# Regrouping the token-major mixer projections of a two-layer encoder kernel into pieces of 512, 512, 512 and 192 columns, with two more matrix-product buffers moved and a few orders changed

## The chip, the cores and the metric

The kernel runs on one core of a Trainium2 chip. The metric is the device time of one execution in microseconds (us), smaller is better. All times below are device times or times from one profiled execution.

## The reference

The input is 256 tokens of 1024 features in float32, with 256 memory tokens. Two layers follow one another; each is a token mixer, a cross-attention into the memory tokens and a gated feed-forward block. Cut to what matters here, the mixer is:

```python
proj = h @ w_in                       # 256 x 1024 times 1024 x 3800-odd
(ml_q, ml_k, ml_v, ml_o, ml_g, na_q, na_k, na_v,
 g_q, g_k, g_v, g_g, g_a) = jnp.split(proj, pts, axis=-1)
# six mLSTM heads of 64: ml_h from ml_q, ml_k, ml_v and the gates ml_g
ml_out = head_rms_norm(ml_h, ml_norm_g, 6) * sigmoid(ml_o)
# five neighbourhood-attention heads from na_q, na_k, na_v
# five gated-linear-attention heads from g_q, g_k, g_v, g_a
gla_out = head_rms_norm(gla_h, gla_norm_g, 5) * silu(g_g)
mixed = concat([ml_out, na_out, gla_out]) @ w_out
```

Five of the thirteen parts of `proj` are wanted with tokens on the partitions ("token-major"): `ml_v` and `ml_o` (384 columns each), `na_v`, `g_v` and `g_g` (320 each), 1728 columns in all.

## The kernel before

**Split products.** Every weight and every activation of a large product is held as a high part and a low part, and a product is three TensorE matmuls (high by high, high by low, low by high). A weight *unit* is up to 2048 values per partition. The DMA queue of SyncE (SP) brings it into one of three slots `raw`; ScalarE (ACT, line 1250) rounds it to `whi`; VectorE (DVE, line 1640) subtracts to get `wlo`; TensorE (PE, lines 755 to 757) uses both. SP may load unit u only when the low half of unit u-3 is done (`load`, line 603 is its DMA); ACT may write `whi` of unit u only when TensorE has used unit u-3. The order of units is the list that `layer_units` writes, and SP, ACT, DVE and TensorE all go through it in that order, each at places of its own program written out by hand (`ahead` on ACT and on DVE, `between` on DVE, `ML_FILL` and `NA_FILL` on TensorE).

**Token-major products.** `tm_half` multiplies half of the 1024 input features (unit `a` or `b`, four blocks of 128) for both groups of 128 tokens: 24 matmuls with the activations stationary and n columns moving. `tm_unit` does both halves, 48 matmuls. The pieces are v 384, nv 320, gv 320, o 384 and gg 320 columns.

**The mLSTM heads.** TensorE makes v, then loops `hh` over the six heads. In step hh it does head hh-1's output (`ml_output`, line 963, which waits until DVE has drained `mls{hh-1}`), in even steps the scores of two heads (line 976), and then a *fill*: nq, nk, gk, nv, gv, o. For each head DVE adds decay rows (lines 1798 to 1801, "decay steps" below), ACT takes the exponential (line 1395), DVE multiplies the scores by it (lines 1814 to 1817, "multiply steps") and TensorE can make the output. The decay rows of head 0 come from a TensorE bank; those of heads 1 to 5 make a round trip through memory: SP waits for the scan (`scan_ready`), writes `gA` out (line 636), waits for `rows_out`, and reads a broadcast row back for each head (line 640). This block stands in SP's loop ahead of the load of unit `nva`:

```python
if name == "nva":
    sp.wait_ge(scan_ready, l + 1)
    sp.dma_start(a["rows"][l], gA[:, :]).then_inc(rows_out, 16)
    sp.wait_ge(rows_out, 16 * (l + 1))
    for hh in range(1, MLH):
        ...
        sp.dma_start(decay_row(hh), ...).then_inc(rows_in[hh], 16)
```

DVE's step for head hh from 1 on begins with `dve.wait_ge(rows_in[hh], ...)`.

**After the heads.** DVE sums the mLSTM heads (`heads_sum`, lines 1777 to 1782), multiplies the decays (`decayed`, lines 1761 and 1762), and then serves the neighbourhood heads: maxima of `nas` (line 1879), shares (`shares_of`, lines 1861 and 1863), then the split of the first memory-key unit (`xk0` in layer 0, `xk2` in layer 1) and the low halves of the memory tokens (`memory_lo`, line 1676). TensorE makes nas, gg, the transposes `nat0` (line 1002, waits for `shares_of(0)`), and then the key unit, whose first blocks wait for the low half of the weights, for each `memory_lo` and for its bank. The bank is 7, and gg's first tokens (`gg0`) were in it, so it waits for ACT to have drained them. SP issues 16 small copies of `nav` (line 633) ahead of the load of that key unit.

**Further on.** `ga` and `kv` products, then xv0 (memory values) into banks 0 and 1, of which bank 0 held `ga0`, drained by DVE at line 1918. In the cross-attention TensorE does transposes `xt3` (line 1150) between the outputs `xo_1` and `xo_2` (line 1161).

Of the kernel before, what the change touches and what calls it, by code (L numbers as in the profile page):

```python
# [21 lines left out]
P = 128  # L22
# [30 lines left out]
def layer_units(l):  # L53
# [16 lines left out]
    tm("v", "w_in", C_V, ML)  # L70
# [42 lines left out]
ML_FILL = (("nq",), ("nk",), ("gk",), ("nv0", "nv1"), ("gv0", "gv1"), ("o0", "o1"))  # L113
WIDTH = {"v": ML, "nv": NA, "gv": GV, "o": ML, "gg": GV}


def layer_events(l):
# [29 lines left out]
    for h in range(MLH + 1):  # L147
        if h:
            job(f"mlo{h - 1}", 4 + (h - 1) % 2)
        else:  # L150
            job("mlb0", 2)
        if h < MLH and h % 2 == 0:
            job(f"mls{h}", 0)
            job(f"mls{h + 1}", 1)
        if h < MLH and len(ML_FILL[h]) == 1:
            job(ML_FILL[h][0], (7, 6)[h % 2], ML_FILL[h][0])
        elif h < MLH:
            tm(ML_FILL[h][0][:-1], (7, 6))
    for h in range(NAH + 2):
# [8 lines left out]
        if h == 0:  # L168
            tm("gg", (7, 6))
# [10 lines left out]
    job("xv0_0", 0)  # L180
    for i in range(4):
        job(f"go{i}", 2 + i)
    job("xv0_1", 1, "xv0b")
# [9 lines left out]
    for kind, i in XATTN:  # L193
        if kind == "xq":
            job(f"xq{i}", (0, 1, 6, 7)[i], f"xq{i}")
        elif kind != "xq_begun":
# [20 lines left out]
for _l in range(1, DEPTH):  # L217
# [5 lines left out]
         ("xt", 2), ("xs", 3), ("xo_", 0), ("xo_", 1), ("xt", 3), ("xo_", 2), ("xo_", 3))  # L223


def layer_drains(l):
# [8 lines left out]
    for h in range(MLH + 1):  # L235
        if h:
            s.append(f"mlo{h - 1}")
        if h < MLH:
            s += ML_FILL[h]
    for h in range(NAH + 2):  # L240
        if 1 <= h <= NAH:
            s.append(f"nat{h - 1}")
        if h == 0:
            s += ["gg0", "gg1"]
# [54 lines left out]
def build(nc, a, out):  # L299
    with ExitStack() as ctx:  # L300
# [287 lines left out]
        def _(sp):  # L588
# [26 lines left out]
            for gu in range(U):  # L615
# [12 lines left out]
                if name == ("xk2" if l else "xk0") and UNITS[gu - 1][0] == (l, "ggb"):  # L628
                    is_drained(sp, l, "nv1")
                    for b in range(4):  # L630
                        for r in range(GR):
                            o = GW * (r % 2) + KEYS_AT[b]
                            sp.dma_start(nav4[KW * r:KW * r + KW, b, :], nav[o:o + KW, r // 2, :]).then_inc(nav_in, 16)  # L633
# [20 lines left out]
                load(gu)  # L654

# [72 lines left out]
        def _(pe):  # L728
# [10 lines left out]
            for l in range(DEPTH):  # L739
# [148 lines left out]
                def fill(names):  # L888
                    if len(names) == 2:
                        tm_unit(names[0][:-1], names, WIDTH[names[0][:-1]], "n1")  # L890
                    else:
                        fm_unit(names[0], "n1")
# [46 lines left out]
                fm_unit("qk2", "n1")  # L939
                tm_unit("v", ("v0", "v1"), ML, "n1")  # L940
# [25 lines left out]
                for hh in range(MLH + 1):  # L966
# [13 lines left out]
                    if hh < MLH:  # L980
                        fill(ML_FILL[hh])

                is_drained(pe, l, "nk")
                for hh in range(NAH + 2):
# [30 lines left out]
                    if hh == 0:  # L1015
                        tm_unit("gg", ("gg0", "gg1"), GV, "n1")
                    if NA_FILL[l][hh] == (0, 1):
                        fm_blocks("xk0", "mem", [(0, 0, 4), (1, 0, 4), (0, 4, KT), (1, 4, KT)], True)
                    else:
                        for i in NA_FILL[l][hh]:  # L1020
                            if l and i == 6:
                                fm_blocks("xk3", "mem", [(0, 0, 4)], halves=l + 1)
# [104 lines left out]
                for kind, hh in XATTN:  # L1127
# [23 lines left out]
                    else:  # L1151
                        pe.wait_ge(xv_lo_ready, TT * (l + 1))
                        pe.wait_ge(xpt_hi_ready, XH * l + hh + 1)
                        free(f"xo_{hh}")
                        for i, (value, share) in enumerate(((xvh, xpth), (xvl, xpth), (xvh, xptl))):
                            if share is xptl:
# [6 lines left out]
                    last.then_inc(te_done, 1)  # L1163
# [50 lines left out]
        def _(act):  # L1214
# [45 lines left out]
            for l in range(DEPTH):  # L1260
# [24 lines left out]
                def take(nm):  # L1285
# [10 lines left out]
                    elif nm[0] == "o":  # L1296
                        drain(A(eo[:, int(nm[-1]), :], b[:, 0:ML], ACT.Tanh, scale=0.5))
                    elif nm[:2] == "gg":
                        t = int(nm[-1])
                        A(gg[:, t, :], b[:, 0:GV], ACT.Copy)  # L1300
                        drain(A(eg[:, t, :], b[:, 0:GV], ACT.Tanh, scale=0.5))
                    else:
                        drain(A((nav if nm[:2] == "nv" else gv)[:, int(nm[-1]), :], b[:, 0:GV], ACT.Copy))
# [872 lines left out]
```

## Time and profile before

| | |
|---|---|
| median of 3 runs | 845.65 us (845.64 to 845.77) |
| the profiled execution, its own time | 846.97 us |
| its span, first to last instruction | 845.2 us |
| TensorE busy | 831.5 us, 6413 matmuls |
| VectorE busy | 612.2 us |
| ScalarE busy | 494.1 us |
| granted TensorE clock, mean | 0.998 |

Times within the profile count from the start of the span. Busy time of TensorE counts pipelined matmuls from start to modelled end, so back-to-back matmuls overlap and the distance between two starts, not the duration, is what one costs. An instruction of DVE or ACT overlaps the next by some 0.08 to 0.1 us too. "Idle before, releaser" names what ended the idle time of an engine just before an instruction.

### The profile page before, as it was taken

To read this page: it belongs to the slowest core of one execution; us is meant where nothing else is said; L and a number is where in the kernel's file an instruction comes from. 1 tells how busy PE (TensorE), PEld (TensorE's weight loads), DVE (VectorE), ACT (ScalarE), POOL (GpSimd) and SP (SyncE) were. 2 spreads that over 40 slices of the span, in tenths; PEclk is the share of its full clock that TensorE was granted. 3 is DMA by queue.
4 is the path that set the end of the run, shared out by engine and by line. 5 is a ranking of instruction groups with operands and counts; after the bars stand their busy time and mean duration, and the time that the engine had idled before them with its cause. 6 is when DMAs were issued, how large, how long until landed. Compare 5 with 4: busy or idle time off the path is not lost.

```text
span 845.2 us, 15174 instructions
## 1 busy us (share of the span) xinstructions
PE 831.5 (98%) x6413; PEld 774.2 (92%) x6413; DVE 612.2 (72%) x849; ACT 494.1 (58%) x693; POOL 19.4 (2%) x39
## 2 busy tenths in 40 slices
PE   8999999999999999999999999999999999999997
PEld 8999998889899999999999999888998999999996
DVE  5898877769757656656576988886776676767665
ACT  7955764578566444445568656745855654444534
POOL 5000001000000000000000000010000000000000
PEclk9999999999999999999999999999999999999999
DMA  9776654535337565565447556436526456564551
GB/s 325 238 128 229 220 190 151 181 122 195 127 124 239 181 205 177 196 199 199 151 127 253 140 173 219 138 121 244 167 83 193 157 199 198 176 226 160 189 174 50
DMA packets 112972, 151.40 MB, mean 179 GB/s; under 512 B 3784, under 2 KB 92808, under 8 KB 112904
## 3 DMA queue, kind: packets, MB, share of 16 engines
q1 hardware_dynamic: 112760, 150.16, 53.9%
q8 instruction: 51, 0.84, 0.4%
q10 hardware_dynamic: 144, 0.26, 0.1%
q14 instruction: 17, 0.14, 0.0%
HBM read 147.92 MB, written 1.18 MB: 176 GB/s over the span
## 4 chain that ended last, share of the span: by engine, by line
PE 89%; DVE 4%; ACT 2%; DMA 2%; SPq 1%; issue 1%; ACTq 0%
PE bank L755 25%; PE bank L756 24%; PE bank L757 24%; PE bank L837 5%; PE bank L880 3%; PE bank L963 2%; PE bank L902 1%; SPq L633 1%; ACT whi L1250 1%; PE bank L1143 1%; DVE wlo L1640 1%; DMA raw<-in_w_in 1%; PE bank L976 1%; PE bank L821 1%; PE bank L1161 1%
## 5 line engine op out<-in xcount | busy, mean ns | idle before, releaser
L1640 DVE TENSOR_TENSOR wlo<-raw,whi 128x2048 fp32r<-128x2048 f32 (+3 forms) x141 | 300.9, 2139 | 98.2 <-ACT whi L1250 97.3
L1250 ACT ACTIVATE whi<-raw 128x2048 fp32r<-128x2048 f32 (+3 forms) x144 | 257.4, 1790 | 53.4 <-PE bank L757 39.2
L755 PE MATMUL bank<-yhi,whi 128*128 128x256 f32 x688 | 190.6, 277 | 0.0
L756 PE MATMUL bank<-ylo,whi 128*128 128x256 f32 x688 | 190.3, 277 | 0.0
L757 PE MATMUL bank<-yhi,wlo 128*128 128x256 f32 x688 | 190.3, 277 | 0.0
L756 PEld LDWEIGHTS bank<-ylo,whi 128*128 128x128 f32 x688 | 129.4, 188 | 0.8
L755 PEld LDWEIGHTS bank<-yhi,whi 128*128 128x128 f32 x688 | 129.2, 188 | 0.9
L757 PEld LDWEIGHTS bank<-yhi,wlo 128*128 128x128 f32 x688 | 129.2, 188 | 0.0
L755 PE MATMUL bank<-whi,xhi 128*128 128x512 f32 (+2 forms) x256 | 90.0, 351 | 2.2 <-DVE arena L1918 2.2
L757 PE MATMUL bank<-whi,xlo 128*128 128x512 f32 (+2 forms) x256 | 88.5, 346 | 0.0
L756 PE MATMUL bank<-wlo,xhi 128*128 128x512 f32 (+2 forms) x256 | 88.4, 345 | 0.0
L755 PE MATMUL bank<-xhi,whi 128*128 128x256 f32 x288 | 82.3, 286 | 1.5 <-DVE xlo L1676 0.9
L756 PE MATMUL bank<-xlo,whi 128*128 128x256 f32 x288 | 80.3, 279 | 0.0
L757 PE MATMUL bank<-xhi,wlo 128*128 128x256 f32 x288 | 80.3, 279 | 0.0
L756 PE MATMUL bank<-wlo,fhi 128*128 128x512 f32 x176 | 69.0, 392 | 0.0
L755 PE MATMUL bank<-whi,fhi 128*128 128x512 f32 x176 | 68.9, 391 | 0.0
L757 PE MATMUL bank<-whi,flo 128*128 128x512 f32 x176 | 68.6, 390 | 0.0
L1575 ACT ACTIVATE arena<-bank,pcols 128x256 f32<-128x256 f32 x44 | 22.4, 560 | 75.7 <-DVE bank L2051 42.1
L755 PEld LDWEIGHTS bank<-xhi,whi 128*128 128x128 f32 x288 | 54.2, 188 | 5.0 <-issue 3.1
L755 PEld LDWEIGHTS bank<-whi,xhi 128*128 128x128 f32 x256 | 48.1, 188 | 7.0 <-issue 3.1
L756 PEld LDWEIGHTS bank<-xlo,whi 128*128 128x128 f32 x288 | 54.4, 189 | 0.0
L757 PEld LDWEIGHTS bank<-xhi,wlo 128*128 128x128 f32 x288 | 54.2, 188 | 0.0
(317 smaller groups left out, 1387.6 us busy)
## 6 DMA issues: line engine op xcount, KB each, us to landing
raw<-in_w_up SPq DMA_DIRECT2D x44, 1024.0 KB, 5.0
raw<-in_w_down SPq DMA_DIRECT2D x22, 1024.0 KB, 4.8
raw<-in_w_in SPq DMA_DIRECT2D x10, 1024.0 KB, 6.2
raw<-in_w_xk SPq DMA_DIRECT2D x8, 1024.0 KB, 5.2
raw<-in_w_xv SPq DMA_DIRECT2D x8, 1024.0 KB, 4.9
raw<-in_w_out SPq DMA_DIRECT2D x8, 1024.0 KB, 5.0
raw<-in_w_xq SPq DMA_DIRECT2D x8, 1024.0 KB, 5.2
raw<-in_w_xo SPq DMA_DIRECT2D x8, 1024.0 KB, 4.9
```

The source lines that it names most:

```text
L633: sp.dma_start(nav4[KW * r:KW * r + KW, b, :], nav[o:o + KW, r // 2, :]).then_inc(nav_in, 16)
L755: mm(o, s_hi, m_hi, start=first, stop=False, skip_group_check=True)
L756: mm(o, s_hi, m_lo, start=False, stop=False, skip_group_check=True)
L757: return mm(o, s_lo, m_hi, start=False, stop=last, skip_group_check=True)
L821: last = mm(bank(name, 2, T)[:, f, :], w[:, k, f * P:f * P + P], x[:, k, :], start=k + i + f == 0, stop=k == KT - 1 and i == 2, skip_group ...
L837: last = mm(bank(name, 2, T)[:, f, :], w[:, k, f * P:f * P + P], x[:, k, :], start=k + i + f == 0, stop=k == KT - 1 and i == 2, skip_group ...
L880: last = mm(bank(names[t])[:, 0:n], x[:, k, t * P:(t + 1) * P], w[:, k, :], start=k + i == 0, stop=False, skip_group_check=True)
L902: last = nc.tensor.transpose(turned_bank(l, group, k)[:, t * P:(t + 1) * P], src[:, t, k * P:(k + 1) * P], ident[:])
L963: last = mm(o[:, t, d, :], w[:, c:c + P], mv[:, jt, g, :], start=i == 0, stop=i == len(src) - 1)
L1250: A(weight(whi, gu), raw[:, gu % RING, 0:SIZE[gu]], ACT.Copy).then_inc(hi_done, 1)
L1575: last = A(fy[:, p % 2, f, :], bank(f"fa{p}", 2, T)[:, f, :], ACT.Identity, scale=pcol[:, RA + RB_W + 22 + j:RA + RB_W + 23 + j], bias=pco ...
L1640: tt(weight(wlo, gu), raw[:, gu % RING, 0:SIZE[gu]], weight(whi, gu), ALU.subtract).then_inc(lo_done, 1)
```

## The change

The 1728 token-major columns are cut anew. v takes 384 columns of `ml_v` and the first 128 of `ml_o`; nv takes `na_v` and the next 192 of `ml_o`; gv takes the last 64 of `ml_o`, `g_v` and the first 128 of `g_g`; gg is the 192 columns that are left. Three pieces have 512 columns, one has 192, and the units are v, nq, nk, gk, gg, nv, gv. TensorE does gg after gk in step 2 of the heads, one half of nv in steps 3 and 4, the first half of gv in step 5, and its second half in step 0 of the neighbourhood heads. ACT drains the parts of each bank to where they belong. The split orders on ACT and DVE follow the units; `between` is gone; DVE splits the first key unit before it begins the neighbourhood heads. In layer 0 qk2 begins on half of its low weights. SP issues the `nav` copies behind the load of the first key unit. xv0 goes to banks 6 and 7. In the cross-attention the first product of `xo_2` is done ahead of `xt3`.

```diff
     def tm(name, m, c, n, halves="ab"):
+        tm_of(name, m, halves, (c, n))
+
+    def tm_of(name, m, halves, *columns):
         for half in halves:
-            u.append(((l, name + half), m, 4 * "ab".index(half), 4, ((c, n),)))
+            u.append(((l, name + half), m, 4 * "ab".index(half), 4, columns))
...
-    tm("v", "w_in", C_V, ML)
+    tm("v", "w_in", C_V, 512)
     fm("nq", "w_in", (C_NQ, 256))
     fm("nk", "w_in", (C_NK, 256))
     fm("gk", "w_in", (C_GK, P))
-    tm("nv", "w_in", C_NV, NA)
-    tm("gv", "w_in", C_GV, GV)
-    tm("o", "w_in", C_O, ML)
-    tm("gg", "w_in", C_GG, GV)
+    tm("gg", "w_in", C_GG + P, 192)
+    tm_of("nv", "w_in", "ab", (C_NV, NA), (C_O + P, 192))
+    tm_of("gv", "w_in", "ab", (C_O + 320, 64), (C_GV, GV + P))
...
-ML_FILL = (("nq",), ("nk",), ("gk",), ("nv0", "nv1"), ("gv0", "gv1"), ("o0", "o1"))
+ML_FILL = ("nq", "nk", "gk", "nva", "nvb", "gva")
...
-    job("xv0_0", 0)
+    job("xv0_0", 6)
...
-    job("xv0_1", 1, "xv0b")
+    job("xv0_1", 7, "xv0b")
...
-         ("xt", 2), ("xs", 3), ("xo_", 0), ("xo_", 1), ("xt", 3), ("xo_", 2), ("xo_", 3))
+         ("xt", 2), ("xs", 3), ("xo_", 0), ("xo_", 1), ("xo_begun", 2), ("xt", 3), ("xo_", 2), ("xo_", 3))
...                 # SP
-                if name == ("xk2" if l else "xk0") and UNITS[gu - 1][0] == (l, "ggb"):
-                    is_drained(sp, l, "nv1")
-                    ... 16 copies of nav
                 load(gu)
+                if name == ("xk2" if l else "xk0") and UNITS[gu - 1][0] == (l, "gvb"):
+                    is_drained(sp, l, "nv1")
+                    ... 16 copies of nav
...                 # TensorE
-                fm_unit("qk2", "n1")
-                tm_unit("v", ("v0", "v1"), ML, "n1")
+                fm_blocks("qk2", "n1", [(0, 0, 4), (1, 0, 4)], halves=2 if l == 0 else 0)
+                fm_blocks("qk2", "n1", [(0, 4, KT), (1, 4, KT)])
+                tm_unit("v", ("v0", "v1"), 512, "n1")
...
                         fill(ML_FILL[hh])
+                    if hh == 2:
+                        tm_unit("gg", ("gg0", "gg1"), 192, "n1")
...
-                        tm_unit("gg", ("gg0", "gg1"), GV, "n1")
+                        tm_half("gv", "b", ("gv0", "gv1"), 512, "n1")
...                 # ACT
-                ahead = (("gk",), ("nva",), ("nvb",), ("gva", "gvb"), ("oa", "ob"), ("gga", "ggb"))
+                ahead = ("gk", "gga", "ggb", "nvb", "gva", "gvb")
...
+                        if hh == 3:
+                            take("gg0")
+                            take("gg1")
+                        split_hi(ahead[hh])
...
+                        if hh == 2:
+                            split_hi("nva")
+                        if hh == 4:
+                            take("nv0")
+                            take("nv1")
+                split_hi("xk2" if l else "xk0")
...                 # DVE
-                ahead = ("nk", "gk", "nvb", "gva", "oa", "gga")
-                between = {4: "gvb", 5: "ob"}
+                ahead = ("nk", "gga", "ggb", "nvb", "gva", "gvb")
...
+                        split_lo("nva")          # in step 2, after the bias
                 heads_sum(0, MLH - 1)
                 decayed()
-                split_lo("ggb")
+                split_lo("xk2" if l else "xk0")
...
                             shares_of(g)
-                        split_lo("xk2" if l else "xk0")
                         memory_lo("mem", l, range(KT))
```

## Rows read from the trace of the kernel before

**Rows 1.** The page's busy times by engine.

```profile
PE 831.5 (98%) x6413; PEld 774.2 (92%) x6413; DVE 612.2 (72%) x849; ACT 494.1 (58%) x693; POOL 19.4 (2%) x39
```

**Rows 2.** Waits of TensorE over the span: total us, times, longest.

```profile
PE bank L755 <- DVE arena L1918: 2.2, 2, 1.1
...
PE bank L755 <- DVE xlo L1676: 0.9, 1, 0.9
...
PE bank L755 <- DVE wlo L1640: 0.6, 1, 0.6
PE bank L1150 <- DVE tmb L1985: 0.4, 2, 0.2
```

**Rows 3.** TensorE in order of time: start, us, instruction; parts of four products.

```profile
39.16 0.33 PE L755 MATMUL bank<-whi,xhi 128*128 128x384 f32 x1
...
44.88 0.33 PE L755 MATMUL bank<-whi,xhi 128*128 128x384 f32 x1
...
60.46 1.45 PE L963 MATMUL bank<-mv,arena 128*128 128x65 f32 x12
...
67.85 0.31 PE L755 MATMUL bank<-whi,xhi 128*128 128x320 f32 x1
...
74.01 0.31 PE L755 MATMUL bank<-whi,xhi 128*128 128x320 f32 x1
...
136.64 0.40 PE L755 MATMUL bank<-whi,xhi 128*128 128x512 f32 x1
...
142.78 0.39 PE L755 MATMUL bank<-whi,xhi 128*128 128x512 f32 x1
```

**Rows 4.** VectorE in order of time, layer 0: `nk` split, head 1, both ends of the stretch.

```profile
51.57 2.28 DVE L1640 TENSOR_TENSOR wlo<-raw,whi 128x2048 fp32r<-128x2048 f32 x1
...
55.63 0.48 DVE L1798 SCALAR_TENSOR_TENSOR arena<-arena,gt,mlm 128x256 f32<-128x256 f32 x1
...
58.69 0.41 DVE L1817 SCALAR_TENSOR_TENSOR arena<-bank,arena 128x256 f32<-128x256 f32 x1
...
101.29 2.29 DVE L1640 TENSOR_TENSOR wlo<-raw,whi 128x2048 fp32r<-128x2048 f32 x1 [1.86 <-ACT whi L1250]
103.49 3.26 DVE L1676 SCALAR_TENSOR_TENSOR xlo<-memT,pcols,xhi 128x256 fp32r<-128x256 f32 x8
```

**Rows 5.** VectorE's waits, layer 0, 55 to 104 us: total, times, longest.

```profile
DVE arena L1814 <- ACT arena L1395: 2.7, 3, 0.9
DVE wlo L1640 <- ACT whi L1250: 2.1, 2, 1.9
```

**Rows 6.** The same view, layer 1, 481 to 529 us.

```profile
DVE wlo L1640 <- ACT whi L1250: 2.9, 3, 2.1
```

**Rows 7.** VectorE in order of time, layer 1: `nk` split, both ends of the stretch.

```profile
477.89 2.28 DVE L1640 TENSOR_TENSOR wlo<-raw,whi 128x2048 fp32r<-128x2048 f32 x1
...
481.94 0.48 DVE L1798 SCALAR_TENSOR_TENSOR arena<-arena,gt,mlm 128x256 f32<-128x256 f32 x1
...
528.46 3.25 DVE L1676 SCALAR_TENSOR_TENSOR xlo<-memT,pcols,xhi 128x256 fp32r<-128x256 f32 x8
```

**Rows 8.** DMA issues by line, layer 0: KB each, us from issue to landing.

```profile
arena<-decay_rows SPq DMA_DIRECT2D x2, 256.0 KB, 5.5
...
decay_rows<-arena SPq DMA_DIRECT2D x1, 64.0 KB, 2.0
```

**Rows 9.** The same view, layer 1.

```profile
arena<-decay_rows SPq DMA_DIRECT2D x2, 256.0 KB, 5.2
decay_rows<-arena SPq DMA_DIRECT2D x1, 64.0 KB, 3.9
```

**Rows 10.** ScalarE in order of time, layer 0.

```profile
96.44 0.40 ACT L1426 ACTIVATE arena<-arena,nmax 128x128 f32<-128x128 f32 x1 [0.88 <-DVE nmax L1879]
...
99.34 1.91 ACT L1250 ACTIVATE whi<-raw 128x2048 fp32r<-128x2048 f32 x1 [1.25 <-DMA raw<-in_w_xk]
...
102.76 0.42 ACT L1300 ACTIVATE gg<-bank 128x320 f32<-128x320 f32 x1
```

More of the change, by code:

```diff
@@ L154, in layer_events @@
             job(f"mls{h + 1}", 1)
[L155 to L158, printed above, removed]
+        if h < 3:
+            job(ML_FILL[h], (7, 6)[h % 2], ML_FILL[h])
+            if h == 2:
+                tm("gg", (6, 3))
+        elif h < MLH and h != 4:
+            used(ML_FILL[h])
+        elif h == 4:
+            job("nv0", 7)
+            job("nv1", 6, "nvb")
     for h in range(NAH + 2):
@@ L168, in layer_events @@
         if h == 0:
-            tm("gg", (7, 6))
+            job("gv0", 7)
+            job("gv1", 6, "gvb")
         for i in NA_FILL[l][h]:
@@ L237, in layer_drains @@
             s.append(f"mlo{h - 1}")
-        if h < MLH:
-            s += ML_FILL[h]
+        if h < 3:
+            s.append(ML_FILL[h])
+        elif h < 5:
+            s += [["gg0", "gg1"], ["nv0", "nv1"]][h - 3]
     for h in range(NAH + 2):
@@ L243, in layer_drains @@
         if h == 0:
-            s += ["gg0", "gg1"]
+            s += ["gv0", "gv1"]
         s += [f"xk{i // 2}" for i in NA_FILL[l][h] if i % 2]
@@ L654, in _ @@
                 load(gu)
+                if name == ("xk2" if l else "xk0") and UNITS[gu - 1][0] == (l, "gvb"):
+                    is_drained(sp, l, "nv1")
+                    for b in range(4):
+                        for r in range(GR):
+                            o = GW * (r % 2) + KEYS_AT[b]
+                            sp.dma_start(nav4[KW * r:KW * r + KW, b, :], nav[o:o + KW, r // 2, :]).then_inc(nav_in, 16)
             lo_is(sp, DEPTH - 1, "mem", KT - 1)
@@ L1151, in _ @@
                     else:
+                        begun = hh == 2 and kind == "xo_"
                         pe.wait_ge(xv_lo_ready, TT * (l + 1))
                         pe.wait_ge(xpt_hi_ready, XH * l + hh + 1)
-                        free(f"xo_{hh}")
+                        if not begun:
+                            free(f"xo_{hh}")
                         for i, (value, share) in enumerate(((xvh, xpth), (xvl, xpth), (xvh, xptl))):
+                            if kind == "xo_begun" and i or begun and not i:
+                                continue
                             if share is xptl:
@@ L1380, in _ @@
                     is_filled(act, l, f"v{t}")
-                    drain(A(mv[:, t, :, 0:DH], bank(f"v{t}")[:, 0:ML].rearrange("p (h d) -> p h d", d=DH), ACT.Copy))
+                    A(mv[:, t, :, 0:DH], bank(f"v{t}")[:, 0:ML].rearrange("p (h d) -> p h d", d=DH), ACT.Copy)
+                    drain(A(eo[:, t, 0:P], bank(f"v{t}")[:, ML:512], ACT.Tanh, scale=0.5))
                 split_hi("nk")
@@ L1429, in _ @@
                     if hh == 0:
-                        split_hi("xk2" if l else "xk0")
-                        is_used(act, l, "gga")
+                        is_used(act, l, "gva")
                         if l == 0:
@@ L1434, in _ @@
                         memory_hi("mem", l, range(4))
-                        take("gg0")
-                        is_used(act, l, "ggb")
+                        take("gv0")
+                        is_used(act, l, "gvb")
                         memory_hi("mem", l, range(4, KT))
                         split_hi("xk3" if l else "xk1")
-                        take("gg1")
+                        take("gv1")
                     for i in NA_FILL[l][hh]:
@@ L1713, in _ @@
                 conv(0)
+                if l == 0:
+                    half_lo("qk2", 0)
                 is_filled(dve, l, "gp")
@@ L1719, in _ @@
                 if l == 0:
-                    split_lo("qk2")
+                    half_lo("qk2", 1)
                 if l:
```

58 lines of the change are left out of this document (28 added, 30 removed).

## Prediction

> **What bounds the kernel now.** I read the busy times first, then TensorE's waits, then VectorE and the SyncE queue in order of time through the mixer, because that is where the edits are. TensorE is busy 831.5 of 845.2 us [rows 1] and its waits are few: 2.2 us on `ga0`'s bank at the memory values (once in each layer), 0.9 us at the first memory low half in layer 0, 0.6 us at qk2, 0.4 us at `xt3` [rows 2]. So there is little to win: 4.1 us if all of them go. The other thing to see is how near VectorE is. In the mLSTM heads of layer 0 it waits 2.7 us for exponentials (three of five heads, 0.9 each) and 2.1 us for high halves, 1.9 of it for the key unit [rows 4, 5]; in layer 1 2.7 again and 2.9 [rows 6]. All else of those 48 and 46.5 us is work. TensorE and VectorE run abreast there, and 5 us more on VectorE's chain is 5 us more on TensorE.
>
> **TensorE's own time.** Between starts, 33 matmuls of 384 columns take 5.72 us (0.173 each), 42 of 320 take 6.16 (0.147), 27 of 512 take 6.14 (0.227) [rows 3]. Before, one of each piece costs 2 x 0.173 + 3 x 0.147 = 0.787 us, after 3 x 0.227 = 0.682 plus the 192 columns. No row has 192. By columns alone from 320 it is below 0.09. The nearest row with few columns is the head output: 12 matmuls of 65 columns, each with a fresh 128-column stationary operand, take 1.45 us, less one pipelined tail some 0.11 apiece [rows 3]; a matmul that short is held by something other than its columns. I take 0.11. Then one of each piece is 0.792, and 48 of them in two layers come to +0.5 us; by columns it would be -1.5. Either way the 96 matmuls saved give next to nothing.
>
> The Trainium skill (TensorE: Matmul & The Clock Gate, "Back-to-back issue gap") has a warm matmul start N/2.4 + 2.5 ns after the one before it, 82.5 ns for 192 columns; the sum of this part by it would be some 2 us less for the two layers. The rows of 512 columns stand at 227 ns where it says 216, so the rows go first.
>
> What moves is the place: v grows by 48 x (0.227 - 0.173) = 2.6 us, and everything up to the heads' end comes later by that. Qk2's half split gives 0.6 back in layer 0.
>
> **The decay rows.** This is the large term. SyncE's block that writes the rows and reads them back stands at the load of `nva`. Before, `nva` followed `gk`, whose load has long been allowed, so the block waited only for the scan. After, the loads of `gga` and `ggb` stand ahead of it. A load waits for the low half three units back: `ggb` waits for that of `nk`, which VectorE makes after head 0's multiply steps, just before it wants the rows of head 1. VectorE's order is not changed there, so the rows now start when they are almost due.
>
> Layer 0: `nk` is done at 51.57 + 2.28 = 53.85 before [rows 4]. VectorE's first decay step needs TensorE's `gt` and `mlb0` behind v; v ends 2.6 - 0.6 = 2.0 later, and VectorE had 0.5 of slack (its split of nq ended after them), so `nk` is done at 55.3. Add 0.5 for the issue of `ggb`, 2.0 for the write and 5.5 for the first broadcast read [rows 8]: 63.3. Head 1's decay step stood at 55.63 [rows 4]: +7.6 us. From there to the end of its multiply steps are 58.69 + 0.41 - 55.63 = 3.5 us [rows 4], so TensorE gets head 1's scores at 66.8, and wants them at 60.46 + 1.9 = 62.4 [rows 3]: a wait of about 4.5 us at line 963, the first thing to look for. Layer 1: `nk` at 480.17 [rows 7] plus 2.1, plus 0.5, 3.9 and 5.2 [rows 9] is 491.9 against 481.94 [rows 7]: +9.9. The write took 2.0 in one layer and 3.9 in the other; with both short the sum is 1.9 less, with both long 1.9 more.
>
> **VectorE from head 1 to the memory low halves.** Does it catch up? Before, it hid the exponential of heads 4 and 5 behind a split (`between`); that is gone, +2 x 0.9. Each step has now one unit of 2048, and ACT makes its high half only after the exponential and the copy of the head's output: some 0.3 for a drain and 1.9 for the high half [rows 10] against 1.1 of multiply steps, so VectorE waits 1.0 more in steps 4 and 5, and in step 3, where ACT drains gg0 and gg1 first (four instructions of some 0.3), 2.2. Together 5 x 0.9 + 2 x 1.0 + 2.2 = 8.7 us of waits, where there were 5.0 in layer 0 (2.7, 2.1 and 0.2 for nas) and 5.8 in layer 1. Nine splits instead of thirteen and 1024 fewer columns (v took them) save 1.2. So +2.5 in layer 0, where the 1.9 us wait for the key unit's DMA goes away, since its load is no longer behind the 16 copies; and +1.7 in layer 1. The key unit's split also comes ahead of the neighbourhood maxima: the shares that `nat0` needs are late by the same chain, so TensorE will stand at line 1002 and again at the key unit, some 4 us and then 1 to 2.
>
> Last, the key product goes to bank 7, where gv0 now lies instead of gg0. From the first nas exponential at 96.44 ACT has 1.6 us of exponentials, then the memory high halves (1.6, from 101.2, the end of the key unit's high half, to the drain of gg0 at 102.76) [rows 10], then four drains of about 0.3 instead of two: 4.4 us. VectorE has its first memory low half 3.4 us after the same point. So +1.0 in each layer.
>
> Sum at the first key matmul: layer 0 7.6 + 2.5 + 1.0 = 11.1; layer 1 9.9 + 1.7 + 1.0 - 0.4 (there the low half was ready 0.4 before TensorE came, 528.46 + 0.41 [rows 7] against the key unit's start) = 12.2. TensorE's lateness from v and its +0.5 are inside it, because VectorE arrives later still.
>
> **What is won.** The memory values in bank 6 need not wait for `ga0`: -2.2 us [rows 2]; TensorE waits for nothing behind that product before, so I take it that the wait isn't moved; if it is, this is nothing. `xo_begun` fills `xt3`'s wait: 0.4 idle and the pipeline's refill, -0.6. Qk2's 0.6 and the key unit's 0.9 are swallowed above. The `nav` copies come some 10 us later than before, and TensorE too; I cost them at nothing, and a wait at line 994 would show that wrong.
>
> 23.3 - 2.8 = +20.5 us. On the profiled span 845.2 + 20.5 = 865.7; its own time lies 1.8 above the span and 1.3 above the median, so I add to the median: 845.65 + 20.5 = 866.
>
> **Rivals.**
> *The rows aren't late* (the block's order costs nothing, because the reads land in time). Then the chain is late only by VectorE's new waits and the bank: 2.5 + 1.7 + 2.0, and part of v's 2.6: some +6 - 2.8 + 2.5, 851. Against it: 7.5 us of DMA between two VectorE steps 1.8 us apart. Chance 0.07.
> *VectorE isn't the bound: faster.* If SyncE's write went out with the scan as before and VectorE's waits were covered by TensorE's 2.6 us of later start, only the waits of rows 2 would count: 845.65 - 4.1, 841.5. It decides if VectorE's chain grows by under 2.6 us a layer where I have 10. Chance 0.05.
> *The clock falls in the new waits.* The longest wait of rows 2 is 1.1 us; now there are four of 4 to 6. If the granted clock goes from 2.4 to 1.2 GHz in one, the matmuls behind it cost double for a while. The ones after head 1 are hidden by VectorE; those behind the key unit's wait aren't: with 24 of them slow 2.7 us, with 48 5.4 in each layer: 871 (869 to 877). Chance 0.2.
> The Trainium skill (the same page, Part 1, the HAM clock gate) says that an idle stretch throttles TensorE to half its clock and a busy stretch has to bring it back; no row here shows a fall.
> *192 columns run slow.* If such a product ran at four times its columns, 0.32 us each, 48 x 0.21 = 10 us a layer in step 2, of which the late chain hides 2: 882. No row excludes it. Chance 0.08.
>
> **Numbers.** The forecast has 0.57 and its own range, by the write's landing and a microsecond for each of the waits, is 862 to 870. The remaining 0.03 is anything else. The range for 8 in 10 leaves out the faster case, the slow 192 and most of the case at 851: 853 to 874. A difference of 0.2% (1.7 us) is about what a measurement of this kernel can tell from none. Faster 0.05, same 0.02, slower 0.93.
>
> **What would show it.** After: a wait of TensorE at line 963 in head 1 of both layers, 4 to 6 us; VectorE waiting at line 1798 on the row DMA some 6 us; SyncE's line 636 issued right after the second load of gg, 10 us later than the scan; waits at line 1002 and at the key unit; none at line 755 on line 1918; 192-column matmuls 0.11 us apart. It is wrong if the rows land before head 1, or if VectorE, once late, makes up for it before the key unit, which needs some 5 us of its waits to vanish in each layer.

## The result, and the profile of the changed kernel

The changed kernel takes 876.38 us (median of 5 runs, 875.34 to 878.58) against 845.65 for the kernel before (5 runs beside it, 845.52 to 846.99): ratio 1.0366, 95% interval 1.0349 to 1.0383, slower by 30.7 us. The forecast was 866, slower by 20.5, with a range up to 874. The direction and the late decay rows held, the size did not. One execution of the experiments below, the profiled one of a2_key_back, ran the whole span at a granted clock of 0.753 (1041.78 us); it is left out.

TensorE's waits over the span of the changed kernel, beside [rows 2]: total us, times, longest.

```profile
PE bank L973 <- DVE arena L1847: 10.2, 2, 5.2
PE bank L1014 <- DVE arena L1894: 6.3, 2, 4.0
PE bank L1083 <- issue: 3.4, 2, 2.6
PE bank L764 <- ACT eg L1326: 2.1, 2, 1.2
```

These four are the longest kinds of wait; the four of [rows 2] came to 4.1 us. L973 is the head output (L963 before), L1014 the first neighbourhood transpose, L764 a split product, here the first key unit on gv0's bank. L1083 is the kv product; "issue" means that the profile shows nothing that TensorE waited for. ([rows 2] leaves out some waits of before: with them there were 7.7 us, 1.9 of it one wait for GpSimd's queue, which the changed kernel has too.) TensorE is busy 12 us longer than in [rows 1] for 96 fewer matmuls:

```profile
PE 843.7 (96%) x6317; PEld 772.9 (88%) x6317; DVE 612.6 (70%) x846; ACT 493.8 (56%) x705; POOL 21.7 (2%) x39
```

The decay rows, in order of time: SyncE's queue, then VectorE and TensorE (layer 0 first, then layer 1). They answer to [rows 4, 7, 8].

```profile
54.83 0.37 SPq L612 DMA_DIRECT2D raw<-in_w_in  x1
55.24 0.52 SPq L639 DMA_DIRECT2D decay_rows<-arena  x1
58.49 0.90 SPq L643 DMA_DIRECT2D arena<-decay_rows  x2
```

```profile
52.52 2.28 DVE L1671 TENSOR_TENSOR wlo<-raw,whi 128x2048 fp32r<-128x2048 f32 x1
...
63.68 0.49 DVE L1830 SCALAR_TENSOR_TENSOR arena<-arena,gt,mlm 128x256 f32<-128x256 f32 x1 [7.15 <-DMA arena<-decay_rows]
...
504.82 0.48 DVE L1830 SCALAR_TENSOR_TENSOR arena<-arena,gt,mlm 128x256 f32<-128x256 f32 x1 [6.96 <-DMA arena<-decay_rows]
```

```profile
67.20 2.82 PE L973 MATMUL bank<-mv,arena 128*128 128x65 f32 x12 [5.25 <-DVE arena L1847]
...
508.35 2.82 PE L973 MATMUL bank<-mv,arena 128*128 128x65 f32 x12 [4.99 <-DVE arena L1847]
```

The low half of `nk` ends at 54.8, the load of `ggb` goes out at 54.83, the write of the rows right behind it, and head 1's decay step starts at 63.68; the forecast had 63.3, and 66.8 for TensorE. Then see the duration of the 12 products: 2.82 us where [rows 3] have 1.45. That is the clock. Windows of TensorE with its granted clock (the first number behind the engines):

```profile
66.00:76.00 10.00, 8.79 (x40) 7.85 (x41) 9.09 (x18) 3.31 (x6) 0.00 (x0) 0.51 0.61 140
117.00:125.00 8.00, 8.00 (x66) 7.67 (x66) 6.19 (x8) 6.81 (x13) 0.00 (x0) 0.81 0.26 78
503.00:515.00 12.00, 7.01 (x33) 5.86 (x32) 8.36 (x17) 3.46 (x7) 0.00 (x0) 0.62 0.67 215
555.00:562.00 7.00, 6.05 (x47) 5.71 (x48) 4.84 (x14) 5.72 (x17) 0.00 (x0) 0.76 0.48 185
```

The clock fell from 2.4 to 1.2 GHz twice in each layer: in the wait at head 1, and around the key unit, in layer 0 in the wait before it (0.53 from 113 to 117 us), in layer 1 at 557.0, when its products had run at full clock for 1.0 us. The rival that had this at 0.2 came true. (The Trainium skill, TensorE: Matmul & The Clock Gate, Part 1, says that an idle stretch throttles TensorE to half its clock. By that rule, the trace agrees at head 1, with 1.00 from 62 to 65 us, early in the wait, and 0.51 from 66 to 76; at layer 1's key unit the fall came 1.0 us behind the end of the waits.)

Where TensorE stands, as starts of its products (from the order of time of both kernels; "late" is after less before):

| product | before | late, layer 0 | before | late, layer 1 |
|---|---|---|---|---|
| v | 37.59 | -1.2 | 463.89 | +13.9 |
| head 1's output | 60.46 | +6.7 | 486.75 | +21.6 |
| first key matmul | 104.12 | +12.8 | 529.26 | +26.7 |
| second transpose | 109.75 | +14.35 | 532.22 | +28.2 |
| kv | 133.22 | +14.35 | 547.58 | +28.1 |
| memory values xv0 | 135.18 | +14.3 | 549.55 | +29.8 |
| last matmul | | | 838.91 | +29.4 |

The new stops inside the kv product, layers 0 and 1, in order of time:

```profile
146.43 1.21 PE L1061 MATMUL bank<-arena 32*64 32x64 f32 x80
147.57 0.77 PE L1083 MATMUL bank<-gv,arena 64*32 64x64 f32 x47
149.17 0.34 PE L1083 MATMUL bank<-gv,arena 64*32 64x64 f32 x13 [0.83 <-issue]
...
575.70 0.76 PE L1083 MATMUL bank<-gv,arena 64*32 64x64 f32 x44
579.03 0.35 PE L1083 MATMUL bank<-gv,arena 64*32 64x64 f32 x16 [2.57 <-issue]
```

In both places TensorE stops between two tiny matmuls of one product that need the same things. The page's DMA queues have a kind "instruction":

```profile
q8 instruction: 50, 0.82, 0.4%
```

50 packets for 2 x 6317 instructions of TensorE and its weight loads is one per 126 matmuls (51 for 6413 before, the same share), so I take these packets to be TensorE's instructions. The DMA view of 576 to 577 us, where the long stop begins, holds one of them (packets, MB, share):

```profile
q8 instruction: 1, 0.02, 5.8%
```

That TensorE ran out of instructions there is a theory which the trace suggests; a4_shift tests it.

### The profile page after: what moved, and what is told of

Same layout as the page of the kernel before. It is cut to its first block, busy times and chain, and to the rows that moved or that the text cites. A ratio compares the mean times of both kernels' runs of the same rounds, so it can differ in the third digit from the quotient of the medians.

```text
span 874.6 us, 14991 instructions
## 1 busy us (share of the span) xinstructions
PE 843.7 (96%) x6317; PEld 772.9 (88%) x6317; DVE 612.6 (70%) x846; ACT 493.8 (56%) x705; POOL 21.7 (2%) x39
## 4 chain that ended last, share of the span: by engine, by line
PE 85%; DVE 4%; DMA 4%; issue 3%; ACT 3%; SPq 0%; DVEq 0%; ACTq 0%
PE bank L764 23%; PE bank L765 23%; PE bank L766 23%; PE bank L846 5%; PE bank L889 2%; PE bank L1177 1%; ACT whi L1267 1%; PE bank L1155 1%; DMA arena<-decay_rows 1%; PE bank L911 1%; DMA raw<-in_w_in 1%; DMA decay_rows<-arena 1%; DMA raw<-in_w_few 1%; DVE wlo L1671 1%; PE bank L830 1%
## 5 line engine op out<-in xcount | busy, mean ns | idle before, releaser
L1671 DVE TENSOR_TENSOR wlo<-raw,whi 128x2048 fp32r<-128x2048 f32 (+2 forms) x136 | 297.9, 2195 | 104.5 <-ACT whi L1267 103.8
L1267 ACT ACTIVATE whi<-raw 128x2048 fp32r<-128x2048 f32 (+2 forms) x140 | 256.6, 1836 | 46.5 <-PE bank L766 39.2
L764 PE MATMUL bank<-yhi,whi 128*128 128x256 f32 x688 | 190.6, 277 | 0.0
L764 PEld LDWEIGHTS bank<-yhi,whi 128*128 128x128 f32 x688 | 129.2, 188 | 0.9
L764 PE MATMUL bank<-xhi,whi 128*128 128x256 f32 x288 | 85.1, 296 | 2.1 <-ACT eg L1326 2.1
L764 PE MATMUL bank<-whi,xhi 128*128 128x512 f32 (+1 forms) x224 | 85.2, 380 | 0.0
L766 PE MATMUL bank<-whi,xlo 128*128 128x512 f32 (+1 forms) x224 | 83.6, 373 | 0.0
L765 PE MATMUL bank<-wlo,xhi 128*128 128x512 f32 (+1 forms) x224 | 83.6, 373 | 0.0
L764 PE MATMUL bank<-whi,fhi 128*128 128x512 f32 x176 | 68.9, 391 | 0.0
L764 PEld LDWEIGHTS bank<-xhi,whi 128*128 128x128 f32 x288 | 57.0, 198 | 6.4 <-issue 3.4
L765 PEld LDWEIGHTS bank<-xlo,whi 128*128 128x128 f32 x288 | 57.3, 199 | 0.0
L766 PEld LDWEIGHTS bank<-xhi,wlo 128*128 128x128 f32 x288 | 57.0, 198 | 0.0
L764 PEld LDWEIGHTS bank<-whi,xhi 128*128 128x128 f32 x224 | 42.2, 188 | 8.3 <-issue 1.0
```

The source lines that it names most:

```text
L764: mm(o, s_hi, m_hi, start=first, stop=False, skip_group_check=True)
L765: mm(o, s_hi, m_lo, start=False, stop=False, skip_group_check=True)
L766: return mm(o, s_lo, m_hi, start=False, stop=last, skip_group_check=True)
L1267: A(weight(whi, gu), raw[:, gu % RING, 0:SIZE[gu]], ACT.Copy).then_inc(hi_done, 1)
L1671: tt(weight(wlo, gu), raw[:, gu % RING, 0:SIZE[gu]], weight(whi, gu), ALU.subtract).then_inc(lo_done, 1)
```

## The experiments

All are compared with the kernel before on the same chip, whose median was 846.75 to 846.89 in these runs. The changed kernel was not run again beside them, and the kernel before was 1.2 us slower here than beside it (845.65), so a difference to its 876.38 carries that much doubt; where it matters, the traces are compared. Line numbers move by a few lines from kernel to kernel. "Changed kernel" is the one with the whole diff.

| kernel | median us | ratio to before (95%) |
|---|---|---|
| a1_rows_early | 863.14 | 1.0190 (1.0171 to 1.0209) |
| b1_rows_late | 864.45 | 1.0200 (1.0181 to 1.0219) |
| a3_busy | 875.48 | 1.0334 (1.0309 to 1.0360) |
| a4_shift | 874.16 | 1.0315 (1.0295 to 1.0334) |
| a2_key_back | 863.96 | 1.0199 (1.0178 to 1.0221) |
| a5_decays_behind | 858.68 | 1.0146 (1.0130 to 1.0161) |
| a6_decays_behind_2 | 854.92 | 1.0095 (1.0081 to 1.0109) |
| a7_busy_key | 869.17 | 1.0263 (1.0247 to 1.0279) |
| a8_high_half_first | 861.90 | 1.0174 (1.0117 to 1.0231) |
| b2_values_6_7 | 845.24 | 0.9973 (0.9953 to 0.9993) |
| b4_three_small | 844.55 | 0.9973 (0.9965 to 0.9982) |
| b5_small_and_decays | 846.60 | 0.9999 (0.9990 to 1.0008) |

### The rows, taken out and put in

```diff
 # a1_rows_early, on the changed kernel
-                if name == "nva":
+                if name == "gga":
                     sp.wait_ge(scan_ready, l + 1)
 # b1_rows_late, on the kernel before
-                if name == "nva":
+                if name == "gva":
                     sp.wait_ge(scan_ready, l + 1)
```

> The changed kernel with SyncE's write and reads of the decay rows ahead of the load of gga, where they follow gk's load as they did before. My theory, that the late rows carry most of the 30.7 us: head 1's decay step no longer waits on the row DMA (7.1 us in layer 0), TensorE's wait at the head output (5.2 and 5.0 us) falls under 1, and with it go the stretches at half clock that follow it. The time comes down by 17 to 22 us, to 854 to 860. Rival, that VectorE's new waits and the key unit's order set the pace whatever the rows do: the time stays above 868.

> The kernel before with SyncE's rows block moved behind the loads of nva and nvb, two units later, which is the same place relative to the low half of nk as in the changed kernel; nothing else is changed. My theory: nk is done at 53.85, plus 0.5, 2.0 and 5.5 gives 61.9 for head 1's decay step, +6.2 us, in layer 1 some 7 to 8; VectorE can win back little, so the time rises by 11 to 16 us, to 857 to 862. Rival, that VectorE, once late, makes up for it out of the 5 us that it waits for others in that stretch: under 852.

One line of SyncE gives back 13.2 us of the 30.7, and the same line alone costs the kernel before 17.6. In a1_rows_early the rows go out at 43.66 and head 1's decay step stands at 56.54, without a wait. In b1_rows_late the waits on VectorE and TensorE are those of the changed kernel, 6.3 us at each head output, again with products of twice the duration behind them:

```profile
62.81 0.48 DVE L1798 SCALAR_TENSOR_TENSOR arena<-arena,gt,mlm 128x256 f32<-128x256 f32 x1 [7.77 <-DMA arena<-decay_rows]
```

```profile
66.34 2.83 PE L963 MATMUL bank<-mv,arena 128*128 128x65 f32 x12 [6.27 <-DVE arena L1817]
```

Against that, VectorE won back little: the first key matmul is 7.3 us late in layer 0. Both results lie outside what I gave, a1 by 3 us above and b1 by 2.5. The two effects don't add: the rows cost 17.6 alone and 13.2 on top of the rest. a1 loses 3.5 us of its gain to other things than the rows: its stops in the kv product are 4.7 us and not 3.4, the key unit of layer 0 loses 2.3 at half clock and not 1.5, and behind a stop in layer 1 another 1.4 go at half clock. In layer 1 its clock stays full behind head 1, where the changed kernel's falls; that is part of what the line gives back (see the clock below). What a1 has left, 16 us, begins at these waits of TensorE:

```profile
PE bank L1014 <- DVE arena L1894: 6.3, 2, 4.0
PE bank L1083 <- issue: 4.7, 2, 3.5
PE bank L764 <- ACT eg L1326: 2.1, 2, 1.2
```

### The stops without a releaser

```diff
 # a4_shift, on the changed kernel
+                    if hh == 2 and l == 0:
+                        free("mlo1")
+                        for _ in range(48):
+                            mm(bank("mlo1")[:, 0:32], PAIR["n1"][0][:, 0, 0:P], PAIR["n1"][0][:, 0, 0:32], start=True, ...)
                     if hh:
                         ml_output(hh - 1)
```

> The changed kernel with 48 tiny products of 32 columns ahead of head 1's output in layer 0 alone, inside a wait of 5 us, so that they cost nothing there; they shift where TensorE's instruction loads fall in its stream by 48 products. Theory, that the stops inside the kv product (0.83 us in layer 0, 2.57 in layer 1, with no releaser) are a load of instructions that arrives late in the run of 140 tiny products: both stops change by more than 0.5 us or move to another product of the run, and the time by up to 2 us either way. Rival, that a bank, an operand or the clock stops it there: both stops stay as long as they are, within 0.2, at the same product.

Both stops are gone; the kv product of both layers runs through:

```profile
147.84 0.88 PE L1087 MATMUL bank<-gv,arena 64*32 64x64 f32 x60
```

```profile
576.10 0.87 PE L1087 MATMUL bank<-gv,arena 64*32 64x64 f32 x60
```

Now xv0 comes 1.15 us nearer to kv than before in each layer, which is the gain of 1.1 that the prediction had counted. In layer 1 nothing was changed but how many instructions stand ahead, so it is the place of an instruction load in the stream. Two more readings of the traces fit. The changed kernel, a1_rows_early and a8_high_half_first give TensorE the same stream, and in all three the product stops at the same matmul (behind 47 of its 60 in layer 0, 44 in layer 1), for 0.83 to 1.19 and 2.30 to 3.50 us. And each of the ten stops of this kind in seven kernels ends 1.2 to 1.5 us after the transfer of an instruction packet has ended (in layer 1 of the changed kernel it ends at 577.6, and TensorE goes on at 579.03). 140 tiny matmuls of 15 ns use up a packet's worth of instructions in 2 us; that a packet asked for in that stretch comes too late is my reading, since no record shows when it is asked for. Of the 3.9 us that xv0 comes nearer to kv in the two layers together, the time fell by 2.2.

The 48 products also measured something: they took 6.64 us in the wait here, the last 2.9 of them at half clock, and 5.28 us at full clock in a5_decays_behind below, 0.110 each for 32 columns.

### The clock

```diff
 # a3_busy, on the changed kernel
+                    if hh == 2:
+                        free("mlo1")
+                        keep_clock(20, bank("mlo1"))     # products of 128 columns on the identity
                     if hh:
                         ml_output(hh - 1)
...
+                        free(f"nat{g}")
+                        if g == 0:
+                            keep_clock(10, bank("nat0"))
                         pe.wait_ge(npn_ready, NAH * l + g + 1)
-                        free(f"nat{g}")
 # a7_busy_key: nothing at head 1, and keep_clock((18, 10)[l], bank("nat0"))
```

> The changed kernel with 20 products of 128 columns on the identity ahead of head 1's output and 10 ahead of the first neighbourhood transpose in each layer, where TensorE stands idle for 5 and for 2 to 4 us; their results are overwritten. Theory of the clock: the granted clock stays at full level behind both places, and of the four stretches at half clock those behind the key unit cost 1.5 us in each layer, the others are hidden by VectorE: 2 to 4 us faster than the changed kernel, 872 to 874. Rival, that half clock is hidden everywhere: 876 as the changed kernel, within 1.

> The changed kernel with 18 (layer 0) and 10 (layer 1) products of 128 columns on the identity ahead of the first neighbourhood transpose, in its waits of 4.0 and 2.3 us; nothing at head 1. Theory, that the fall of the granted clock behind the key unit's wait costs 1.5 us in each layer: TensorE takes from the first key matmul to the second transpose 5.6 us in layer 0 and 3.0 in layer 1, as before the change, where the changed kernel took 7.2 and 4.5; the time falls by 3 us if the stops inside the kv product stay as they are (they can move by 2 us either way, since the instruction loads shift). Rival, that the stretch is slow for another reason: 7.2 and 4.5 stay.

a3_busy gained only 0.9 by the medians, less than I gave. Its fill at head 1 did keep the clock (1.00 from 62 to 72 us). In layer 0 that bought nothing, since VectorE is the bound there: from head 1's decay step to the first memory low half VectorE takes 52.1 us in the changed kernel and 52.4 in a3. In layer 1 it bought 2.5 us: 50.0 became 47.5 (504.82 to 554.80, and 504.58 to 552.03), and VectorE's wait of 1.25 us for TensorE's scores is gone. a1_rows_early, whose clock is full there too, takes 48.1, and a7_busy_key, which leaves head 1 alone, 49.6. So half clock behind head 1 is hidden in layer 0 and costs 2.5 us in layer 1. I had expected it to be hidden in both. ScalarE's rows show how it gets through: it drains the slow gk product before it makes `nva`'s high half, and in layer 1 it stands waiting for that product (first row, changed kernel), so the high half begins at 517.79, in a3 at 515.64. In layer 0 it waits for gk too, but a3, without that wait, only waits for the load of `nva` instead (second row, a3_busy), which lands no earlier.

```profile
517.51 0.38 ACT L1307 ACTIVATE gk<-bank 128x256 f32<-128x256 f32 x1 [1.79 <-PE bank L766]
```

```profile
78.15 1.92 ACT L1272 ACTIVATE whi<-raw 128x2048 fp32r<-128x2048 f32 x1 [2.88 <-DMA raw<-in_w_in]
```

Why the time hardly shows it: ahead of the key unit of layer 0 ten products did not fill the wait and the clock fell (0.79 from 117 to 125); the 60 more products (each is two matmuls in the trace) made one stop of 4.2 us in the kv product out of the two; and behind that stop the clock was at half again, which took 1.3 us more from xv0 of layer 1 to the end.

```profile
117.00:125.00 8.00, 7.35 (x50) 7.34 (x50) 6.19 (x9) 6.83 (x14) 0.00 (x0) 0.79 0.32 108
```

a7_busy_key fills that wait better. The same two windows as above:

```profile
117.00:125.00 8.00, 8.00 (x80) 7.66 (x79) 6.19 (x8) 6.51 (x12) 0.00 (x0) 1.00 0.35 103
555.00:562.00 7.00, 7.00 (x82) 6.47 (x81) 5.18 (x18) 6.58 (x19) 0.00 (x0) 1.00 0.03 10
```

80 matmuls where there were 66, and 82 for 47. From the first key matmul to the second transpose it takes 5.8 us in layer 0 and 2.9 in layer 1, where the changed kernel took 7.2 and 4.5: 3.0 us of half clock. Its shift of the instructions took the stops away as well (xv0 is 1.15 us nearer to kv again, 3.9 us with what the stops had cost), and 3.0 + 3.9 is nearly the whole of its 7.2 us, which has the doubt of 1.2 us said above.

### What is left with the rows in time

```diff
 # a2_key_back, on a1_rows_early: DVE
                 decayed()
-                split_lo("xk2" if l else "xk0")
...
                             shares_of(g)
+                        split_lo("xk2" if l else "xk0")
 # ACT: split_hi of the same unit behind the exponentials of nas
 # a5_decays_behind, on a2_key_back, with the 48 products of a4_shift: DVE
                 heads_sum(0, MLH - 1)
-                decayed()
...
                         memory_lo("mem", l, range(KT))
+                        decayed()
 # a6_decays_behind_2: the 48 products are 32 by 32 on the identity (96 matmuls in the trace)
 # a8_high_half_first, on a1_rows_early: ACT
+                        split_hi(ahead[hh])
                         if hh == 3:
                             take("gg0")
                             take("gg1")
-                        split_hi(ahead[hh])
```

> The kernel of a1_rows_early (863.1 us, rows in time), with the first key unit's split put back where it was: on VectorE behind the shares, on ScalarE behind the exponentials of the neighbourhood heads. My theory, that TensorE's waits of 4.0 and 2.3 us at the first transpose and what comes behind it are one and the same lateness of VectorE's chain: the wait at the transpose falls to under 2 us, but the first key matmul starts at the same time within 1 us, less the 0.9 and 1.2 us on gv0's bank, since ScalarE drains it 2 us earlier: 861 to 862. Rival, that the order of the key unit is what costs in the regrouped kernel: 857 or less.

> The kernel of a2_key_back, with two changes more: the 48 tiny products that move the instruction loads, and VectorE's four decay products of the linear attention (2.7 us) moved behind the memory low halves. If VectorE's chain up to the memory low halves is what TensorE waits for, the first key matmul starts some 2.7 us earlier in each layer than in a2_key_back and the stops inside the kv product (4.7 us together) go: 9 us less than a2_key_back, 851 to 854. If TensorE itself or the DMA is the bound there, the gain is only the stops': 856 to 858.

> The kernel of a5_decays_behind with the 48 shifting products made of 32 by 32 on the identity instead of a 128 by 128 stationary operand, since those cost 0.11 us each and head 1 has no wait there to hide them. Theory: TensorE's 5.3 us at head 1 of layer 0 go, all else stays: 858.7 less 4.5 to 5.3, 853 to 854.5. Rival, that VectorE's chain is late there anyway: 857 or more.

> The kernel of a1_rows_early (863.1 us) with ScalarE's four drains of gg0 and gg1 behind the high half of nvb in step 3 of the heads, not ahead of it. Theory, that each wait of VectorE for a high half in the heads goes straight into TensorE's time: VectorE's wait in step 3 (1.81 us in layer 0) falls by some 1.2 us, the first key matmul of each layer comes 0.8 to 1.2 us earlier, and the kernel takes 861 to 862. Rival, that the drains then delay the exponential of head 4 and the high half behind it: the wait only moves, 863 within 0.7.

a2_key_back is no faster than a1_rows_early (its three runs are 861.5, 864.0 and 865.7, and the one trace of it is of the execution that is left out). So the order of the key unit is not what costs, as far as these runs can tell; I had expected 1 to 2 us.

a5_decays_behind and a6_decays_behind_2 show that VectorE's length up to the memory low halves is. a6 takes 854.9 us, 9.0 less than a2_key_back and 0.4 above what I gave; the stops are gone in it, 4.7 us in a1, and in layer 1 the first key matmul is 1.6 us later than layer 0 left it (+8.4 against +6.8), where a1 has 4.0. That is the decays' part, 2.4 us, in the layer that has no fill in it. a5 came 4.7 us above what I gave, and above its rival's 858 too, because its 48 products had no wait to hide in there and took their 5.28 us from TensorE:

```profile
61.80 5.43 PE L980 MATMUL bank<-xhi 128*128 128x32 f32 x48
67.08 2.52 PE L973 MATMUL bank<-mv,arena 128*128 128x65 f32 x12
```

a6's still took 3.2 us there. VectorE remains late by the memory low halves, 3.9 us in both:

```profile
PE bank L764 <- DVE xlo L1711: 3.9, 2, 2.6
```

a8_high_half_first: VectorE's wait for the high half in step 3 fell from 1.81 us to 0.93, and the first key matmul of layer 0 came 0.9 us earlier, as the theory had it; its four runs scatter from 856.5 to 864.7, so the time by itself decides nothing. In layer 1 nothing is gained between head 1 and the key unit: the first key matmul is 0.8 us earlier there and head 1's decay step had been 1.2 earlier.

```profile
77.75 2.29 DVE L1671 TENSOR_TENSOR wlo<-raw,whi 128x2048 fp32r<-128x2048 f32 x1 [0.93 <-ACT whi L1267]
```

### The small edits on the kernel before

```diff
 # b2_values_6_7
-    job("xv0_0", 0)
+    job("xv0_0", 6)
...
-    job("xv0_1", 1, "xv0b")
+    job("xv0_1", 7, "xv0b")
 # b4_three_small: b2, and from the change xo_begun and the half split of qk2
 # b5_small_and_decays: b4, and decayed() behind memory_lo
```

> The kernel before with only the memory values in banks 6 and 7. Theory of the prediction, that the wait of 2 x 1.1 us on ga0's bank is simply won: 2.2 us faster, 843.5. Rival: the time stays within 0.7 us, because the wait hides one of another kind (instructions loaded late, as in the kv product of the changed kernel), which then shows in its place.

> The kernel before with three edits that don't touch the pieces of the token-major projections: the memory values in banks 6 and 7, the first product of xo_2 ahead of xt3, and qk2 begun on half of its low weights in layer 0. By the prediction's terms 2.2 + 0.6 + 0.6 = 3.4 us faster than before, 842.3; if only the last two hold 1.2, 844.5.

> The kernel of b4_three_small (the pieces as before) with VectorE's four decay products behind the memory low halves. TensorE waited 1.2 us there for the first memory low half in layer 0, so 0.8 to 1.2 us less than b4_three_small, 843.5. Rival, that the late decays stop TensorE at the transposes of kt: no gain, 844.5 or more.

b2_values_6_7 gains 1.6 us. At xv0 it has 1.15 us in each layer, all of it; then layer 1 gives 0.5 back to an instruction load, which the ga0 wait had covered before:

```profile
551.93 0.39 PE L755 MATMUL bank<-whi,xhi 128*128 128x512 f32 x1 [0.46 <-issue]
```

and of the 1.3 us that layer 0 is ahead behind the cross-attention 0.6 are lost again by its end, for which I have no cause. b4_three_small gains 2.3 us, less than the 3.4 by the prediction's terms; at 844.55 us it is the fastest of all. Its ratio is that of b2, whose interval is wider, so the 0.7 us between the two medians is not shown beyond doubt; both beat the kernel before. b5_small_and_decays loses that again: the kv product starts 0.8 us later in layer 0 and 1.3 in layer 1 than in b4. Where TensorE and not VectorE is the bound, moving the decays gains nothing and, as I read it, makes them late for what needs them.

## Why the prediction was right and wrong

| step | forecast | measured |
|---|---|---|
| rows late, layer 0 | +7.6 | +8.05 (63.68 less 55.63) |
| rows late, layer 1 | +9.9 | +9.0 (504.82 less 481.94, less the 13.9 that the layer began late) |
| VectorE's waits and gv0's bank, to the first key matmul | +3.5, +2.3 | +4.8, +1.3 (12.8 in each layer, less the rows, in layer 1 less the 2.5 of the next row) |
| half clock behind head 1 | 0 | 0, +2.5 (a3_busy) |
| half clock behind the key unit | 0 | +1.5, +1.5 (a7_busy_key) |
| memory values at xv0 | -1.1, -1.1 | -0.1, +1.65 |
| xo_begun | -0.6 | -0.8 (0.4 in each layer) |
| sum on the span | +20.5 | +29.4 |

*Right.* The late rows, their place in SyncE's order and their size; TensorE's waits at head 1 (4.5 forecast, 5.25 and 4.99), at the first transpose (about 4: 4.0 and 2.3) and at the key unit (1 to 2: 0.9 and 1.2); the absence of ga0's wait. 48 products of 192 columns take 5.33 us, 0.111 apiece, which is the value chosen; a1 and b1 confirm the rows from both sides.

```profile
76.55 0.25 PE L764 MATMUL bank<-whi,xhi 128*128 128x192 f32 x1
...
81.78 0.27 PE L766 MATMUL bank<-whi,xlo 128*128 128x192 f32 x1
```

The Trainium skill (TensorE: Matmul & The Clock Gate, "Back-to-back issue gap") gives 82.5 ns for 192 columns by its formula, and says beside it that the formula is for an isolated matmul and comes out too low for few columns when each matmul has its own weight load. The trace agrees with that: 111 ns, and 110 for 32 columns, with a fresh 128 by 128 stationary operand each. The prediction quoted the formula without that remark, and the 2 us that it puts on the difference are 96 x 0.0275 = 2.6.

*The step that failed most: the new waits' matmuls were costed at full clock.* The forecast put TensorE in four waits of 4 to 6 us, named "The clock falls in the new waits" as a rival at 0.2, and left it out of the sum. It cost 5.5 us of the 8.9 by which the span was missed: 1.5 in each layer behind the key unit, which a7 gives back, and 2.5 in layer 1 behind head 1, which a3 gives back. The rival's mechanism was right, and its lower price, 2.7 us in each layer, comes to much the same, but partly by luck: it had head 1 hidden by VectorE in both layers, and that is so in layer 0 only.

*The other: "TensorE waits for nothing behind that product before, so I take it that the wait isn't moved".* The -2.2 us of the memory values became +1.6, an error of 3.75 us. It wasn't the bank: b2 shows that the edit does gain 1.15 us in each layer. The change takes 96 matmuls out of the stream, which moves the instruction loads, and one stopped TensorE in the run of 140 tiny products in each layer. a4 and a7 bring the gain back without touching bank or data.

*VectorE's waits were too small by 1.3 us in layer 0,* and too large by 1.0 in layer 1 once the clock's part is taken out. The step counted 8.7 us; in the stretch from 40 to 125 us of layer 0 it waits 7.8 for high halves and 4.6 for exponentials, as forecast:

```profile
DVE wlo L1671 <- ACT whi L1267: 7.8, 6, 2.4
DVE arena L1830 <- DMA arena<-decay_rows: 7.1, 1, 7.1
DVE arena L1844 <- ACT arena L1419: 4.6, 5, 0.9
```

Of the 7.8 us 1.8 come behind the first memory low half, at 120.31 and 123.14; the other 6.0 stand against the 4.2 that were counted. Left out was `nva`'s high half, 2.4 us by itself. Its load is allowed by the low half of `gk`, which VectorE makes from 67.07 on, goes out at 68.31, and the high half is begun at 77.44:

```profile
79.39 2.29 DVE L1671 TENSOR_TENSOR wlo<-raw,whi 128x2048 fp32r<-128x2048 f32 x1 [2.36 <-ACT whi L1267]
```

I had followed the units' loads for the rows' sake and not for their own. Of the 1.8 us that the high halves cost more than counted, 1.3 reached the key unit. One count of the same step was wrong without harm: VectorE makes eight splits where there were ten, not nine for thirteen; the 1024 columns saved are right.

The last 1.3 us is no step: the profiled execution of before lay 1.3 above the median and the one of after on it, so 29.4 on the spans are 30.7 between medians. What stays open: why the key unit's order didn't help by the bank's 2 us (the one trace of a2 can't be used), and how b2 loses some 0.6 us before layer 1.

## What to carry to other kernels

When loads are reordered in a queue, look for what else stands in that queue at a place defined by a load's name: here one `if name ==` carried about half of the loss. A wait like the ones here (5.25, 4.99, 4.0 and 0.9, 2.3 and 1.2 us) that one puts into TensorE's path is to be costed with half clock behind it; that another engine hides it has to be shown for each place, since the same wait was hidden in one layer and not in the other. And where a run of tiny matmuls uses up a packet of instructions in a couple of microseconds, the time of the kernel depends on how many instructions stand ahead of it; an edit far away can cost or win 1 to 4 us, and a few idle products in a wait show whether it does.

## What the runs showed of the hardware

- TensorE's instructions come in packets, one per about 126 matmuls (50 for 6317). A load that falls into tiny matmuls, or just behind them, stops it for 0.4 to 4.2 us (0.83 and 2.57 in the changed kernel, 1.19 and 3.50 in a1, 1.00 and 2.30 in a8, 4.20 in a3; 0.46, 0.45 and 0.39 behind them in b2, b4 and b5), and the profile gives no releaser. The stop ends 1.2 to 1.5 us after the packet's transfer, and neither a4, a5, a6, a7 nor the kernel before has one.
- Such a stop can also bring the clock down. Behind the one of 3.50 us in a1_rows_early it was granted 0.57 on the mean of 564 to 568 us, which made the stretch behind xv0's start 1.4 us longer; behind a3's stop of 4.20 us it was 1.3. Behind the stops of 2.57 us and less it stayed at full level.

```profile
564.00:568.00 4.00, 3.98 (x26) 3.09 (x26) 3.25 (x13) 0.00 (x0) 1.00 (x1) 0.57 0.72 266
```

- Half clock for some microseconds cost 0 us (head 1, layer 0), 2.5 (head 1, layer 1) and 1.5 (key unit, each layer), read from the kernels that keep the clock up there.
- A matmul with a fresh 128 by 128 stationary operand costs 0.11 us at full clock for 32, 65 or 192 columns. In a4_shift the clock fell at 65.6 us in the middle of 48 such products of 32 columns, although they followed one another without a gap.
